# Turning and evicting the next head's query and key between the halves of the weight block, and behind the exponentials, in a two-block decoder kernel on one Trainium2 core

## The chip, the core and the metric

The kernel runs on one core of a Trainium2 chip. The metric is the device time of one execution in microseconds; it was run three times.

## The reference

Two stacks of blocks over 256 tokens of width 1024, in float32. The first stack has two layers. Each normalises its input, multiplies it with a wide weight matrix and computes heads: the even layer 8 differential attention heads (A: two softmaxes of 64 channels each, with ALiBi) and 4 cross attention heads over a memory (X); the odd layer 4 cross attention heads (Y) and 12 forgetting attention heads (C). The gated heads go through an output matrix and are added to the input. The heads that matter here:

```python
s1 = einsum('bhqd,bhkd->bhqk', q1b, k1) * scale + bias        # A, and s2 of the second halves
p1 = softmax(where(causal, s1, -inf)); p2 = softmax(where(causal, s2, -inf))
attn = p1 - lam * p2
o = einsum('bhqk,bhkd->bhqd', attn, v)
s = einsum('bhqd,bhkd->bhqk', qb, k) * scale                  # C
s = s + (cqb[..., :, None] - cum[:, :, None, :])
p = softmax(where(causal, s, -inf))
```

Queries and keys are normalised over the channels and have a gain per channel. The second stack (a recurrent and convolutional mixer, a pooling mixer, cross attention, two gated feed-forward blocks) follows; the change does not touch it.

## The kernel before, in words

All matrix products with weights are done three times over: a weight is split into a high part and a low part (w_hi, w_lo), as the activations are (u_s holds both parts), and high times high, high times low and low times high are summed in PSUM. A weight block (a "unit") is 1 MB. SP's queue loads it into w_raw (line 397), ScalarE copies it in two halves into w_hi (`hi`, line 1267), VectorE subtracts to get w_lo (`lo`, line 1908), and TensorE multiplies it in two halves. There are two buffers, so ScalarE works on block u+2 while TensorE multiplies block u: the first half of w_hi of block u+2 waits for TensorE's first half of block u, the second for its second half.

A unit has one of two forms. `k8_unit` (line 556) has 48 products of 256 columns and fills one bank, which ScalarE evicts at its end (line 1298, with Silu where the columns are a gate). `row_unit` (line 576) has 24 products of 512 columns; two such units make a pair, and their two banks are evicted in the second (line 1322). Both forms take a function `between`, which TensorE calls between the halves. The passes did not use it before the change. In both, a product with its three passes is lines 552, 553 and 554.

The two head passes ("e": heads 0 to 11, A then X; "o": heads 12 to 27, Y then C) run in slots. In the text slots are numbered by the number of their head, so that slots 0 to 16 are the first pass with its tail and slots 12 to 32 the second. In slot s every engine has an order written out by hand, and heads are at different stages:

- TensorE (`attention`, line 851): turn y of head s-5 (line 846), turn the probabilities of s-3 (line 804), scores of s-1 (lines 770 and 771 for A, 775 to 780 for C, 783 for X and Y), values of s-4 (lines 828 to 836), turn query and key of s (`st_turn_qk`, line 745), then the weight block of the slot. The scores wait for `a_qk`, the signal that ScalarE has evicted query and key of their head.
- ScalarE (`attention`, line 1512): y_hi of s-5 (line 1509), copy of the turned probabilities of s-3 (line 1480), squares of s-4 for A heads (line 1491), eviction of query and key of s (`st_qk`, lines 1443 and 1446; X and Y have a query only), first half of w_hi, exponentials of s-1 (`st_exp`, lines 1463, 1467, 1471), bank eviction, second half of w_hi. Exponential and Silu are in different function tables; a change between them is an ACT_TABLE_LOAD.
- VectorE (line 2227): y_lo of s-5 (lines 2196, 2200; waits for y_hi), combination of the probabilities of s-2 (lines 2141 to 2161), second half of w_lo, mask and maxima of s-1 (lines 2115 to 2127), gated head of s-4 (lines 2177, 2186), first half of w_lo.

Of the kernel before, what the change touches and what calls it, by code (L numbers as in the profile page):

```python
# [209 lines left out]
def build_program(nc, t, out):  # L210

    with ExitStack() as ctx:
# [52 lines left out]
        def tv(ap):  # L265
            return ap.rearrange("p (k n) -> p k n", n=SEQ)

        hv = two(h[:, :], D)
        uh, ul, yh_, yl_ = tv(u_hi), tv(u_lo), tv(y_hi[:, :]), tv(y_lo[:, :])
# [278 lines left out]
        def _(pe):  # L548
# [7 lines left out]
            def k8_unit(slot, bk, xh, xl, wait_lo, wait_bank, fresh=None, between=None):  # L556

                for half in range(2):  # L560
                    if fresh is not None:
                        pe.wait_ge(tL, fresh[half])
                    if half == 1 and between is not None:
                        between()
                    pe.wait_ge(lo_done, wait_lo + half)
                    if half == 0 and wait_bank is not None:
                        pe.wait_ge(evacuated, wait_bank)
                    for m in range(2):
                        for k in range(4 * half, 4 * half + 4):
                            a = 2048 * slot + SEQ * k + P * m  # L570
                            mm = passes(bank[bk][:, SEQ * m:SEQ * m + SEQ],
                                        ((w_hi[:, a:a + P], w_lo[:, a:a + P]), (xh[:, k, :], xl[:, k, :])),
                                        half == 0 and m == 0 and k == 0, k == 7)
                    mm.then_inc(half_done, 1)
# [22 lines left out]
            def row_of(name, j, xh, xl, fresh=None, between=None):  # L597

                u, kb = UNIT0[name] + j, BANK0[name] + j - j % 2
                first = j - j % 2  # L600
                row_unit(u % 2, j % 2, (unit_bank(name, first), unit_bank(name, first + 1)), xh, xl, 2 * u + 1,
                         kb - 1 if kb else None, fresh, between)
# [248 lines left out]
            def attention(name):  # L851
                lo, hi = PASS[name]
                for s in range(lo, hi + LAG):
                    for lag, stage in ((5, st_turn_y), (3, st_turn_p), (1, st_scores), (4, st_values), (0, st_turn_qk)):
                        if lo <= s - lag < hi:
                            stage(s - lag)
                    phase, before, count, out_name = BESIDE[name]
                    kind, j = beside(name, s)
                    u = beside_unit(name, s)
                    if kind == "K8":  # L860
                        kb = BANK0[phase] + j
                        if pair_of(phase, j) is None:
                            k8_unit(u % 2, kb % 2, uh, ul, 2 * u + 1, kb - 1)
                        else:
                            row_of(phase, j, uh, ul)
                    elif kind == "DN":
                        if j == 0:
                            pe.wait_ge(evacuated, BANK0[phase] + before + count)
                            pe.wait_ge(a_qk, hi)
                        pe.wait_ge(a_yl, lo + (A_HEADS if name == "e" and j == 0 else 2 * j + 2))  # L870
                        down_phase(out_name, j, 1)
# [178 lines left out]
            u, kb = UNIT0["e_nat"] + 14, BANK0["e_nat"] + 14  # L1050
# [29 lines left out]
            def turn_mem(m):  # L1080
                pe.wait_ge(nrm_ready, 5 + m)
                turn_tile(nrm, m)

            for j in range(2):
                u, kb = UNIT0["ab_t"] + j, BANK0["ab_t"] + j
                k8_unit(u % 2, kb % 2, uh, ul, 2 * u + 1, kb - 1,
                        fresh=(turned("h2", 3), turned("h2")) if j == 0 else None,
                        between=(lambda: turn_mem(0)) if j == 1 else None)
# [163 lines left out]
        def _(act):  # L1252
# [93 lines left out]
            def row_of(name, j, out_, between=None, after=None):  # L1346

                first = j - j % 2
                row_step(UNIT0[name] + j, j % 2, pair_of(name, j), (unit_bank(name, first), unit_bank(name, first + 1)), out_,
                         between=between, after=after)  # L1350
# [84 lines left out]
            def st_qk(g):  # L1435
                kind, hd = HEADS[g]
                if kind == "G":
                    return
                act.wait_ge(a_tr, g + 1)
                if g >= 2:  # L1440
                    act.wait_ge(a_sc, g - 1)
                qg = {"A": 0, "X": 1, "C": 2, "Y": 3}[kind]
                ins = act.activation(qk[g % 2][:, 0:SEQ], bank[TRB][:, 0:SEQ], ACT.Copy, scale=qs[:, qg:qg + 1])
                if kind in "AC":
                    kg = GCOL["ak" if kind == "A" else "ck"]
                    ins = act.activation(qk[g % 2][:, SEQ:512], bank[TRB][:, SEQ:512], ACT.Copy,
                                         scale=gT[:, kg:kg + 1])
                ins.then_inc(a_qk, 1)

            def st_exp(g):  # L1450
                kind, _ = HEADS[g]
                p = g % 2
                act.wait_ge(a_mx, g + 1)
                if kind in "XYG":
                    if g >= 2:
                        act.wait_ge(a_pt, g - 1)
                if g >= 2:
                    act.wait_ge(a_pn, g - 1)
                if kind == "A":
                    parts = [(c, m, Sb[p][:, 384 * c + P * m:384 * c + (P if m == 0 else 384)]) for c in range(2) for m in range(2)]  # L1460
                    for c, m, s in parts:
                        at = 2 * m + c
                        ins = act.activation(s, s, ACT.Exp, bias=nmax[p][:, at:at + 1], accum_out=rsum[p][:, at:at + 1])
                elif kind == "C":
                    for m in range(2):
                        s = Sb[p][:, P * m:P if m == 0 else 384]
                        ins = act.activation(s, s, ACT.Exp, bias=nmax[p][:, m:m + 1], accum_out=rsum[p][:, m:m + 1])
                else:
                    for m in range(2):
                        cs = slice(SEQ * m, SEQ * m + SEQ)  # L1470
                        ins = act.activation(Sb[p][:, cs], bank[SC[p]][:, cs], ACT.Exp, bias=nmax[p][:, m:m + 1],
                                             accum_out=rsum[p][:, m:m + 1])
                ins.then_inc(a_ex, 1)
# [38 lines left out]
            def attention(name):  # L1512
                lo, hi_ = PASS[name]
                for s in range(lo, hi_ + LAG):
                    for lag, stage in ((5, st_y_hi), (3, st_copy_p), (4, st_square), (0, st_qk)):
                        if lo <= s - lag < hi_:
                            stage(s - lag)

                    def exponentials():
                        if lo <= s - 1 < hi_:  # L1520
                            st_exp(s - 1)

                    kind, j = beside(name, s)
                    u = beside_unit(name, s)
                    phase, before, _, _ = BESIDE[name]
                    if kind is None:
                        exponentials()
                        continue
                    if kind == "K8" and pair_of(phase, j) is not None:
                        if name == "o" and j == 14:  # L1530
                            act.wait_ge(qk_ready, 4)
                        out_ = (row_out(eV, j // 2) if name == "e" else row_out(oK[:, :, 1024:], 0) if 18 <= j < 20
                                else row_out(oV, (14, 20, 24).index(j - j % 2)))
                        row_of(phase, j, out_, between=exponentials)
                        continue
                    if kind == "DN":
                        evac = None
                    elif name == "e":
                        evac = copy_out(t_dst(eXZ), 1, ACT.Silu) if j == 12 else \
                            copy_out(t_dst((eBH, eBC, eBB, eBZ)[(j - 4) // 2]), j % 2, ACT.Silu if j >= 10 else ACT.Copy)  # L1540
                    elif j < 14:
                        evac = copy_out(t_dst(oXZ), j - 12, ACT.Silu)
                    else:
                        evac = copy_out(t_dst(oZ), (16, 17, 22, 23, 26, 27).index(j), ACT.Silu)
                    step(u, evac, BANK0[phase] + j, between=exponentials)
# [131 lines left out]
            for j in range(OUT_TAIL["e"], 8):  # L1677
                u = UNIT0["e_out"] + j
# [1125 lines left out]
```

## Time and profile before

| what | value |
|---|---|
| median of 3 runs | 1329.51 us (1328.25 to 1330.42) |
| time of the profiled execution | 1328.74 us |
| its span in the trace | 1326.9 us |
| mean granted TensorE clock | 0.988 |
| busy: TensorE, VectorE, ScalarE | 96%, 68%, 52% of the span |
| chain that ended last | 76% TensorE, 12% VectorE, 5% ScalarE |

Times are read from the start of the span. In a timeline row the first number is the start of an instruction, the second its length; instructions overlap in their engine's pipeline, so the distance from one start to the next is what one occupies. A bracket at the end of a row says how long the engine was idle before it and what ended that.

### The profile page before, as it was taken

The page shows a single profiled execution, that of the slowest core. Times are in us where ns is not written, and L with a number is a line of the kernel's source. Part 1 is how long each engine was busy: PE and PEld are TensorE (multiplying, and loading weights), DVE is VectorE, ACT ScalarE, POOL GpSimd, SP SyncE. Part 2 cuts the span into 40 slices and gives each one's busy share as a digit, 9 for nine tenths or more (in the row PEclk, how much of TensorE's full clock was granted, in tenths as well). Part 3 has the DMA queues.
Part 4 walks back from the last instruction along what each step waited for, and adds up shares of the span by engine and source line. Part 5 has one row for each costly group of instructions (what it writes and reads, how often), then busy time and mean ns, then how long its engine had stood idle before and what let it go on. Part 6 is the DMA issues. An engine that isn't in the chain of part 4 may idle for free.

```text
span 1326.9 us, 19085 instructions
## 1 busy us (share of the span) xinstructions
PE 1273.1 (96%) x7208; PEld 1102.2 (83%) x7208; DVE 898.3 (68%) x1285; ACT 687.5 (52%) x1079; POOL 63.0 (5%) x72
## 2 busy tenths in 40 slices
PE   7999999999899999998989999999999998999997
PEld 6887899887788888897877988888887796888886
DVE  7676776775774655789786747666667646566667
ACT  6555777455567676457335444444443353444442
POOL 1012011000100000000000000000000000000000
PEclk9999999999999999999989999999999999999999
DMA  7655333555453434645335444566654453475652
GB/s 246 218 187 172 127 127 127 185 170 187 134 182 128 128 127 160 213 148 183 98 114 188 150 152 133 203 229 221 206 190 135 153 184 100 130 221 189 190 190 96
DMA packets 138525, 219.57 MB, mean 165 GB/s; under 512 B 3739, under 2 KB 92134, under 8 KB 138454
## 3 DMA queue, kind: packets, MB, share of 16 engines
q1 hardware_dynamic: 135110, 206.68, 47.2%
q0 software_dynamic: 3040, 11.19, 2.7%
q8 instruction: 47, 0.77, 0.2%
q10 hardware_dynamic: 304, 0.73, 0.2%
q14 instruction: 24, 0.20, 0.0%
HBM read 217.54 MB, written 1.05 MB: 165 GB/s over the span
## 4 chain that ended last, share of the span: by engine, by line
PE 76%; DVE 12%; ACT 5%; issue 3%; DMA 2%; POOL 1%; DVEq 0%; SPq 0%; ACTq 0%
PE bank L552 16%; PE bank L554 16%; PE bank L553 16%; PE bank L913 12%; PE bank L915 6%; DVE w_lo L1908 3%; ACT w_hi L1267 2%; DVE h L2065 1%; DVE small L2072 1%; PE bank L788 1%; PE bank L817 1%; PE bank L939 1%; PE bank L804 1%; DVE att L2553 1%; DVE att L1973 1%
## 5 line engine op out<-in xcount | busy, mean ns | idle before, releaser
L1908 DVE TENSOR_TENSOR w_lo<-w_raw,w_hi 128x1024 fp32r<-128x1024 f32 x388 | 471.9, 1224 | 268.8 <-ACT w_hi L1267 262.9
L1267 ACT ACTIVATE w_hi<-w_raw 128x1024 fp32r<-128x1024 f32 x388 | 408.1, 1059 | 431.9 <-PE bank L554 287.7
L913 PE MATMUL bank<-u_s,w_hi 128*128 128x512 f32 x672 | 239.1, 400 | 1.8 <-DVE u_s L2047 1.8
L552 PE MATMUL bank<-w_hi,y_hi 128*128 128x512 f32 x528 | 211.6, 401 | 5.9 <-DVE w_lo L1908 3.5
L554 PE MATMUL bank<-w_hi,y_lo 128*128 128x512 f32 x528 | 207.3, 393 | 0.0
L553 PE MATMUL bank<-w_lo,y_hi 128*128 128x512 f32 x528 | 207.0, 392 | 0.0
L915 PE MATMUL bank<-u_s,w_lo 128*128 128x256 f32 x672 | 189.1, 281 | 0.0
L552 PE MATMUL bank<-u_s,w_hi 128*128 128x256 f32 x544 | 157.4, 289 | 4.7 <-DVE u_s L2047 3.9
L913 PEld LDWEIGHTS bank<-u_s,w_hi 128*128 128x128 f32 x672 | 127.0, 189 | 33.3 <-DVE u_s L2047 2.0
L553 PE MATMUL bank<-u_s,w_hi 128*128 128x256 f32 x544 | 154.6, 284 | 0.0
L554 PE MATMUL bank<-u_s,w_lo 128*128 128x256 f32 x544 | 154.5, 284 | 0.0
L552 PE MATMUL bank<-w_hi,u_s 128*128 128x512 f32 x336 | 134.8, 401 | 10.9 <-DVE w_lo L1908 4.0
L553 PE MATMUL bank<-w_lo,u_s 128*128 128x512 f32 x336 | 132.2, 394 | 0.0
L554 PE MATMUL bank<-w_hi,u_s 128*128 128x512 f32 x336 | 132.0, 393 | 0.0
L915 PEld LDWEIGHTS bank<-u_s,w_lo 128*128 128x128 f32 x672 | 127.6, 190 | 0.7
L552 PEld LDWEIGHTS bank<-w_hi,y_hi 128*128 128x128 f32 x528 | 100.1, 190 | 29.8 <-DVE w_lo L1908 3.5
L554 PEld LDWEIGHTS bank<-w_hi,y_lo 128*128 128x128 f32 x528 | 99.8, 189 | 22.0
L553 PEld LDWEIGHTS bank<-w_lo,y_hi 128*128 128x128 f32 x528 | 100.2, 190 | 19.7
L552 PEld LDWEIGHTS bank<-u_s,w_hi 128*128 128x128 f32 x544 | 104.8, 193 | 6.0 <-DVE u_s L2047 4.6
L553 PEld LDWEIGHTS bank<-u_s,w_hi 128*128 128x128 f32 x544 | 105.0, 193 | 0.1
L554 PEld LDWEIGHTS bank<-u_s,w_lo 128*128 128x128 f32 x544 | 104.9, 193 | 0.0
L552 PEld LDWEIGHTS bank<-w_hi,u_s 128*128 128x128 f32 x336 | 63.8, 190 | 26.8 <-ACT nat L1322 5.5
(302 smaller groups left out, 1588.3 us busy)
## 6 DMA issues: line engine op xcount, KB each, us to landing
w_raw<-in_e_w_in SPq DMA_DIRECT2D x28, 1024.0 KB, 5.1
w_raw<-in_o_w_in SPq DMA_DIRECT2D x28, 1024.0 KB, 5.1
w_raw<-in_ffn_wg SPq DMA_DIRECT2D x22, 1024.0 KB, 5.4
w_raw<-in_ffn_wu SPq DMA_DIRECT2D x22, 1024.0 KB, 5.3
w_raw<-in_ffn_wd SPq DMA_DIRECT2D x22, 1024.0 KB, 4.9
w_raw<-in_ab_w_in SPq DMA_DIRECT2D x12, 1024.0 KB, 5.2
w_raw<-in_e_w_out SPq DMA_DIRECT2D x8, 1024.0 KB, 4.8
w_raw<-in_o_w_out SPq DMA_DIRECT2D x8, 1024.0 KB, 5.3
```

What stands on the lines that cost most here:

```text
L552: pe.matmul(out_ap, ah, bh, start=start, stop=False, skip_group_check=True)
L553: pe.matmul(out_ap, ah, bl, start=False, stop=False, skip_group_check=True)
L554: return pe.matmul(out_ap, al, bh, start=False, stop=stop_, skip_group_check=True)
L788: mm = pe.matmul(bank[SC[pr]][:, SEQ * m:SEQ * m + SEQ], XQT[:, 2 * hd + j, P * m:P * m + P], (KT2 if g < 32 else KT1)[:, 2 * hd + j, :], ...
L804: mm = pe.transpose(bank[PTB][:, dst:dst + P], s[:, src:src + P], ident)
L817: mm = pe.matmul(o[:, SEQ * j:SEQ * j + SEQ], V2[:, k, cs], p[:, SEQ * k:SEQ * k + SEQ], start=(k == 0), stop=(k == 1))
L913: pe.matmul(two(bank[banks[m]][:, :], SEQ), w_hi[:, a:a + P], u_both[:, :, SEQ * k:SEQ * k + SEQ], start=(k == 0), stop=False, skip_group_ ...
L915: mm = pe.matmul(bank[banks[m]][:, 0:SEQ], w_lo[:, a:a + P], uh[:, k, :], start=False, stop=(k == 7), skip_group_check=True)
L939: pe.matmul(o[:, :, ts], w_hi[:, a:a + P], u_both[:, :, SEQ * k + P * tile:SEQ * k + P * tile + P], start=(k == 0 and tile == 0), stop=Fal ...
L1267: act.activation(w_hi[:, at:at + 1024], w_raw[:, at:at + 1024], ACT.Copy).then_inc(hi_done, 1)
L1908: v.tensor_tensor(w_lo[:, at:at + 1024], w_raw[:, at:at + 1024], w_hi[:, at:at + 1024].bitcast(F32), ALU.subtract).then_inc(lo_done, 1)
L1973: mark(v.scalar_tensor_tensor(nrm[:, m], src[:, m], mv[:, m, 0:1], gain, ALU.subtract, ALU.mult))
```

## The change

In TensorE's program of both passes `st_turn_qk` of head s leaves the top of the slot and is called between the two halves of the slot's weight block. In ScalarE's program `st_qk` of head s leaves its place ahead of the first half of w_hi and stands behind the exponentials of head s-1, ahead of the bank eviction and the second half of w_hi. Every slot that turns a head has a weight block of the input projection, so all 28 heads are moved. VectorE's program and the queues of SP and GpSimd are as before.

```diff
--- before.py
+++ after.py
@@ -851,19 +851,26 @@
             def attention(name):
                 lo, hi = PASS[name]
                 for s in range(lo, hi + LAG):
-                    for lag, stage in ((5, st_turn_y), (3, st_turn_p), (1, st_scores), (4, st_values), (0, st_turn_qk)):
+                    for lag, stage in ((5, st_turn_y), (3, st_turn_p), (1, st_scores), (4, st_values)):
                         if lo <= s - lag < hi:
                             stage(s - lag)
+
+                    def next_head():
+                        if s < hi:
+                            st_turn_qk(s)
+
                     phase, before, count, out_name = BESIDE[name]
                     kind, j = beside(name, s)
                     u = beside_unit(name, s)
                     if kind == "K8":
                         kb = BANK0[phase] + j
                         if pair_of(phase, j) is None:
-                            k8_unit(u % 2, kb % 2, uh, ul, 2 * u + 1, kb - 1)
+                            k8_unit(u % 2, kb % 2, uh, ul, 2 * u + 1, kb - 1, between=next_head)
                         else:
-                            row_of(phase, j, uh, ul)
-                    elif kind == "DN":
+                            row_of(phase, j, uh, ul, between=next_head)
+                        continue
+                    next_head()
+                    if kind == "DN":
                         if j == 0:
                             pe.wait_ge(evacuated, BANK0[phase] + before + count)
                             pe.wait_ge(a_qk, hi)
@@ -1512,13 +1519,15 @@
             def attention(name):
                 lo, hi_ = PASS[name]
                 for s in range(lo, hi_ + LAG):
-                    for lag, stage in ((5, st_y_hi), (3, st_copy_p), (4, st_square), (0, st_qk)):
+                    for lag, stage in ((5, st_y_hi), (3, st_copy_p), (4, st_square)):
                         if lo <= s - lag < hi_:
                             stage(s - lag)
 
                     def exponentials():
                         if lo <= s - 1 < hi_:
                             st_exp(s - 1)
+                        if s < hi_:
+                            st_qk(s)
 
                     kind, j = beside(name, s)
                     u = beside_unit(name, s)
```

## Rows read from the trace of the kernel before

**Rows 1.** Windows of both passes: PE, PEld, DVE, ACT, POOL busy (instructions), clock, DMA.

```profile
120.00:235.00 115.00, 112.01 (x806) 101.01 (x805) 83.31 (x165) 84.22 (x201) 11.96 (x17) 1.00 0.40 131
375.00:508.00 133.00, 132.82 (x846) 116.80 (x845) 81.64 (x145) 95.76 (x178) 4.54 (x2) 1.00 0.41 132
```

**Rows 2.** Waits: total us, times, longest; the last row is of the second pass.

```profile
ACT w_hi L1267 <- PE bank L554: 17.4, 13, 2.0
...
PE bank L846 <- DVE att L2186: 0.9, 2, 0.6
...
PEld bank L552 <- ACT nat L1298: 0.8, 2, 0.5
```

**Rows 3.** Timeline of TensorE: block starts with and without transposes ahead.

```profile
122.50 0.28 PE L554 MATMUL bank<-u_s,w_lo 128*128 128x256 f32 x1
...
122.98 0.48 PE L552 MATMUL bank<-w_hi,u_s 128*128 128x512 f32 x1
...
447.34 0.38 PE L833 MATMUL bank<-att,nat 128*128 128x128 f32 x2
...
447.92 0.48 PE L552 MATMUL bank<-w_hi,u_s 128*128 128x512 f32 x1
...
514.01 0.38 PE L833 MATMUL bank<-att,nat 128*128 128x128 f32 x2
514.15 0.47 PE L552 MATMUL bank<-w_hi,y_hi 128*128 128x512 f32 x1
```

**Rows 4.** Timeline of ScalarE: eviction of query and key, first pass.

```profile
180.32 0.48 ACT L1443 ACTIVATE att<-bank,qs 128x256 f32<-128x256 f32 x1 [0.17 <-ACT att L1491]
180.69 0.47 ACT L1446 ACTIVATE att<-bank,gT 128x256 f32<-128x256 f32 x1
```

**Rows 5.** Timeline: slots with a table load, second pass, last C and first Y.

```profile
387.98 1.03 PE L783 MATMUL bank<-mkv,att 128*128 128x256 f32 x4
...
388.21 0.46 ACT L1471 ACTIVATE att<-bank,small 128x256 f32<-128x256 f32 x1
...
503.41 1.28 ACT L1467 ACT_TABLE_LOAD   x1
504.70 0.41 ACT L1467 ACTIVATE att<-att,small 128x128 f32<-128x128 f32 x1
...
505.11 0.49 ACT L1467 ACTIVATE att<-att,small 128x256 f32<-128x256 f32 x1
...
505.28 0.39 PE L775 MATMUL bank<-att 128*128 128x128 f32 x2
```

**Rows 6.** Timeline: a C slot without a table load.

```profile
443.95 0.49 ACT L1467 ACTIVATE att<-att,small 128x256 f32<-128x256 f32 x1
...
445.40 0.39 PE L775 MATMUL bank<-att 128*128 128x128 f32 x2
```

**Rows 7.** Timeline: slot 1 of the first pass and the next block start.

```profile
135.56 0.50 PE L770 MATMUL bank<-att 64*128 64x128 f32 x4
...
137.14 1.06 ACT L1322 ACTIVATE nat<-bank 128x512 f32<-128x512 f32 x2
...
137.86 0.47 PE L552 MATMUL bank<-w_hi,u_s 128*128 128x512 f32 x1 [0.79 <-ACT nat L1322]
```

**Rows 8.** Timeline: one period of slots 7 and 8, first pass.

```profile
184.49 0.40 ACT L1463 ACTIVATE att<-att,small 128x128 f32<-128x128 f32 x1 [1.52 <-DVE small L2120]
...
186.26 0.57 ACT L1298 ACTIVATE nat<-bank 128x512 f32<-128x512 f32 x1
...
188.18 0.48 DVE L2196 SCALAR_TENSOR_TENSOR y_lo<-bank,qs,y_hi 128x256 fp32r<-128x256 f32 x1 [2.08 <-ACT y_hi L1509]
...
192.81 0.68 DVE L2120 TENSOR_REDUCE small<-att 128x2 f32<-128x512 f32 x1
...
193.52 0.40 ACT L1463 ACTIVATE att<-att,small 128x128 f32<-128x128 f32 x1 [1.76 <-DVE small L2120]
...
194.66 1.03 PE L783 MATMUL bank<-mkv,att 128*128 128x256 f32 x4
```

## The prediction

> **What bounds the kernel now.** I first read the windows of the two head passes [rows 1]. The reader is to see that TensorE is busy for 112.01 of 115 us in the first pass and 132.82 of 133 us in the second, at the full granted clock: TensorE's instruction stream sets the time here, so whatever makes TensorE wait is paid in full, and moving its own work about gains nothing by itself. The waits view [rows 2] says what little waiting there is. TensorE waits 0.9 us for VectorE's gated heads (L2186) and, in the second pass, its weight loads 0.8 us for a bank that ScalarE has not emptied. ScalarE waits 17.4 us in the first pass, in 13 pieces, for the first half of a weight block. The evictions of query and key stand today just ahead of that wait. They are hidden in it, and the change takes them out of it. Last I read the timelines slot by slot (a slot is the head work and one weight block).
>
> **TensorE's part.** The transposes (four for an A or C head, two for X and Y) are neither added nor removed. At the boundary, from the last value product to the block's first product, it is 447.34 to 447.92 = 0.58 us with them and 514.01 to 514.15 = 0.14 without: they cost 0.44. Between products of a block: 122.50 to 122.98 is 0.48, less the ordinary 0.12 from one product to the next, 0.36; the first product behind them takes some 0.09 longer than the others, so 0.45 [rows 3]. The difference is 0.01 a slot; I take nothing, with bounds of 0 and 0.1 for each of 28 slots, 0 to 2.8 us. What does change is that the transposes now stand ahead of the next scores instead of behind the last ones, so that the scores come 0.45 later (0.20 with two transposes) after the half of the block that lets ScalarE begin. That is the only cover that the move gives.
>
> **ScalarE's part.** The two evictions start 0.37 apart (180.32, 180.69), so they occupy 0.75 us, and the second ends 0.85 after the first began; with about 0.05 for the semaphore the scores can start 0.90 after the evictions begin [rows 4]. An X or Y head has one: 0.38 of occupancy, 0.53 to the scores. They move past the first half of the weights' high part and past the exponentials, and these now stand behind them in ScalarE's queue: the bank eviction, the second half of the high part, y_hi and the copy of the probabilities. New is that the scores of head s, at the top of slot s+1, follow directly on exponentials plus evictions. Three kinds of slot come out of this.
>
> (a) Slots with a table load ahead of the exponentials, because the block before was gated with Silu. Second pass, last such slot: load at 503.41, exponentials from 504.70 to 505.11 + 0.49 = 505.60, scores possible at 506.50; TensorE gets there at 505.28 + 0.45 = 505.73, so it waits 0.77 [rows 5]. There are five of this kind with C heads, 0.66 to 0.93 each, 4.05 in all by the same subtraction. Two have Y heads; the first: exponentials end at 388.21 + 0.46 = 388.67, scores at 389.20 against 387.98 + 0.20 = 388.18, a wait of 1.02 [rows 5]; the other gives 0.73. Together 5.8. A later block start swallows waits for banks that exist today, 0.5 of the 0.8 in [rows 2]. Second pass: +5.3. C slots without a load have room: exponentials end at 443.95 + 0.49 = 444.44, scores possible at 445.34, TensorE there at 445.40 + 0.45 = 445.85 [rows 6]: no wait, 0.51 to spare.
>
> (b) First pass, slots 1 to 3. In slot 1 the exponentials end at 137.14 (there the bank's eviction starts), so the scores start at 138.04 instead of 135.56 + 0.45 = 136.01: 2.03 of waiting. Behind these scores TensorE waits today for the bank, 0.79 by the row and about 1.0 with what the sequencer adds [rows 7]; that is swallowed, net +1.0. In slots 2 and 3 the exponentials of an A head take 1.77 (184.49 to 186.26) where those of a C head take 0.90 (504.70 to 505.60) [rows 5, 8], so the 0.51 to spare becomes a wait of 0.36: +0.7 for the two. Slot 4 has a longer block and a turned y ahead of its scores: nothing.
>
> (c) First pass, slots 5 to 8: a ring between ScalarE and VectorE. The exponentials start at 184.49 and again at 193.52, a period of 9.03 (three equal ones in a row) [rows 8]. Inside it each step starts as the last ends: exponentials to 186.26, bank eviction, second high half, y_hi; VectorE's y_lo at 188.18, held 2.08 by y_hi; combine, low half, mask and maxima until 192.81 + 0.68 = 193.49; exponentials at 193.52 [rows 8]. The evictions are not in this ring today; the change puts 0.75 us into it. VectorE's 2.08 idle is no cover, for it ends with y_hi, which comes later. So 9.78 a period. The ring is entered 2.0 late (1.7 from (b), and 0.3 because it starts sooner behind the evictions), three periods add 2.25, and the last exponentials, ending today at 193.52 + 1.77 = 195.29, end at 199.5; with one query eviction the scores start at 200.1 instead of 194.66 [rows 8]: 5.4 late in all. One more load slot with an X head, slot 11, gives 0.35 by the way of (a). First pass: +5.8.
>
> Late second halves of w_lo and the weight loads that SP starts behind them move by the same amounts; a block is needed a whole slot later, so they are covered, and POOL's queue has nothing moved past it.
>
> **The sum.** 5.8 + 5.3 = 11.1, and 0.4 of the 0 to 2.8 from TensorE's switching: +11.5. Against the profiled execution's own time, 1328.74 (span 1326.9), that is 1340.2. The median of the runs shown is 0.77 above that execution: 1329.51 + 11.5 = 1341.0.
>
> **A rule against the trace.** A load takes 1.28 and the exponentials begin 1.29 after it began (503.41, 504.70) [rows 5]. The Trainium skill, "ScalarE: Activation LUTs", section "What ACT_TABLE_LOAD costs", counts a drain of some 1.38 us on top of a load of 1.28. By that rule the seven waits of (a) would be 9.7 us longer and the sum an estimated 21; the row shows no such drain, and I go by the row.
>
> **The rivals.**
> Only the load slots pay (chance 0.12): VectorE has slack in the ring that I don't see, and (c) adds nothing beyond (b). Then 1.0 + 0.7 + 0.35 + 5.3 = 7.3, 1336.8. For it: VectorE is idle 2.08 each period. Against: the releaser of that idle is y_hi [rows 8].
> All slots pay (0.08): the 0.51 to spare of a C slot is not there, and the eight C and Y slots without a load wait some 0.4 too, and switching costs 0.1 a slot: 11.1 + 3.2 + 2.8 = 17.1, 1346.6. Against: the arithmetic of [rows 6].
> No measurable change (0.04): the exponentials are released earlier because ScalarE reaches the first high half without the evictions ahead of it, and this makes up for the 0.75. It decides if the first high half waited for ScalarE; but ScalarE waits there for TensorE, 17.4 us in 13 pieces [rows 2]. It would give 1329.5 to 1331.
> Faster (0.03): the ring does not close over y_hi but over VectorE's use of the first high half, so that taking the evictions from ahead of it shortens the ring, and TensorE's present waits, 0.9 for L2186, 0.8 at the banks and 1.0 in slot 1 [rows 2, 7], disappear: 1326.8. It decides if VectorE's long wait in a slot ends with w_hi instead of y_hi.
>
> **How the numbers follow.** The forecast has 0.73. About 0.2%, 2.7 us, is what a measurement of this kernel can tell from no change. The range goes from 1335 (a little below the load-slot case) to 1347 (the case in which all pay). It also holds the sum with each of the 15 waits off by 0.3 us, 4.5, and leaves out only the last two rivals and some of the tails. Slower 0.93, same 0.04, faster 0.03.
>
> **What the changed profile would show.** Right: TensorE's scores (L770, L775, L783) waiting for ScalarE's L1446 or L1443 in slots 1 to 3, 5 to 8 and the load slots, about 0.3 to 2 us each; starts of the exponentials 9.8 apart where they are 9.03; no such wait in C slots without a load; no wait for L2186 left in the first pass; the second pass 5 us longer and the first 6. Wrong: the period still near 9.03, or the scores of the load slots following the transposed probabilities at once. If the scores wait in the plain C slots too, the dear rival holds.

## The result and the profile after

| | before | after |
|---|---|---|
| median of the runs | 1329.97 us (1328.25 to 1331.73, 4 runs) | 1338.99 us (1338.14 to 1340.25, 4 runs) |
| time of the profiled execution | 1328.74 us | 1338.14 us |
| its span | 1326.9 us | 1336.3 us |
| mean granted TensorE clock | 0.988 | 0.989 |

The changed kernel is slower: the ratio of after to before is 1.0072, with a 95% interval of 1.0059 to 1.0085, that is 7.8 to 11.3 us. The forecast was 1341.0 with a range of 1335 to 1347. In a second comparison with more rounds, shown below, the ratio was 1.0084 (1.0070 to 1.0098), 9.3 to 13.0 us.

The waits of TensorE in the changed kernel, total us, times and longest; the first two rows are of the first pass, the last two of the second.

```profile
PE bank L770 <- ACT att L1453: 6.0, 6, 1.9
PE bank L783 <- ACT att L1450: 1.1, 2, 1.0
...
PE bank L775 <- ACT att L1453: 3.0, 5, 0.7
PE bank L783 <- ACT att L1450: 1.3, 2, 0.8
```

Lines 1450 and 1453 are lines 1443 and 1446 of before: the evictions of query and key. In the kernel before none of these waits existed. What stood there, 0.9 us for the gated heads and the waits at the banks [rows 2], is gone from the two windows, except the 1.3 us at the last block start of the first pass. TensorE now waits 7.1 us in the first pass and 4.3 in the second, in 8 and 7 places, always for the eviction of the head whose scores come next. Behind such a wait the first scores of a C, X or Y head also take 0.1 us longer: 516.12 to 516.45 below is 0.33 where 453.51 to 453.74 in a slot without a wait is 0.23. The first scores of an A head take 0.32 in either kernel.

The ring of slots 5 to 8, timeline of ScalarE and VectorE, the period that answers to [rows 8]; the last row is TensorE's scores, which belong near its start:

```profile
186.90 0.40 ACT L1470 ACTIVATE att<-att,small 128x128 f32<-128x128 f32 x1 [1.29 <-DVE small L2129]
...
188.18 0.49 ACT L1470 ACTIVATE att<-att,small 128x256 f32<-128x256 f32 x1
188.68 0.45 ACT L1450 ACTIVATE att<-bank,qs 128x256 f32<-128x256 f32 x1
189.03 0.46 ACT L1453 ACTIVATE att<-bank,gT 128x256 f32<-128x256 f32 x1
189.39 0.58 ACT L1305 ACTIVATE nat<-bank 128x512 f32<-128x512 f32 x1
189.87 1.05 ACT L1274 ACTIVATE w_hi<-w_raw 128x1024 fp32r<-128x1024 f32 x1
190.81 0.46 ACT L1516 ACTIVATE y_hi<-bank,qs 128x256 fp32r<-128x256 f32 x1
...
191.31 0.48 DVE L2205 SCALAR_TENSOR_TENSOR y_lo<-bank,qs,y_hi 128x256 fp32r<-128x256 f32 x1 [2.79 <-ACT y_hi L1516]
...
195.94 0.68 DVE L2129 TENSOR_REDUCE small<-att 128x2 f32<-128x512 f32 x1
...
196.66 0.40 ACT L1470 ACTIVATE att<-att,small 128x128 f32<-128x128 f32 x1 [1.29 <-DVE small L2129]
...
189.54 0.50 PE L770 MATMUL bank<-att 64*128 64x128 f32 x4 [1.23 <-ACT att L1453]
```

Each step of the chain from 186.90 to 196.66 starts as the one before it ends. The exponentials now start 9.76 apart; before it was 9.03. What came in is the two evictions, 188.68 to 189.39 = 0.71. VectorE's idle time ahead of y_lo grew from 2.08 to 2.79, by the same 0.71: it did not shrink to take the evictions in, so it was no cover. The scores at 189.54 start when the second eviction, 189.03 + 0.46 = 189.49, is done.

A load slot, the last of the second pass (it answers to [rows 5]), and a plain C slot ([rows 6]):

```profile
451.58 0.49 ACT L1474 ACTIVATE att<-att,small 128x256 f32<-128x256 f32 x1
...
452.44 0.46 ACT L1453 ACTIVATE att<-bank,gT 128x256 f32<-128x256 f32 x1
...
453.51 0.39 PE L775 MATMUL bank<-att 128*128 128x128 f32 x2
453.74 0.60 PE L776 MATMUL bank<-att 128*128 128x256 f32 x2
...
513.07 1.28 ACT L1474 ACT_TABLE_LOAD   x1
514.36 0.40 ACT L1474 ACTIVATE att<-att,small 128x128 f32<-128x128 f32 x1
514.76 0.49 ACT L1474 ACTIVATE att<-att,small 128x256 f32<-128x256 f32 x1
515.26 0.45 ACT L1450 ACTIVATE att<-bank,qs 128x256 f32<-128x256 f32 x1
515.61 0.46 ACT L1453 ACTIVATE att<-bank,gT 128x256 f32<-128x256 f32 x1
...
515.04 0.49 PE L804 MATMUL bank<-cst,att 128*128 128x128 f32 x3
516.12 0.49 PE L775 MATMUL bank<-att 128*128 128x128 f32 x2 [0.59 <-ACT att L1453]
516.45 0.60 PE L776 MATMUL bank<-att 128*128 128x256 f32 x2
```

In the plain slot the eviction is done at 452.90 and the scores come at 453.51, 0.61 later. Less the 0.05 from an eviction's end to the scores, as at 189.49 and 189.54 above, that is 0.56 to spare, where the forecast had 0.51. In the load slot it is done at 516.07, while TensorE had finished the turned probabilities (three transposes from 515.04) and was idle for 0.59.

**How the loss lies.** The start of each head's scores can be compared between two profiles, counted from the first head of the pass; heads are numbered within their pass. In the first pass the shift grows by 2.05 at head 1 and has fallen to 1.53 at head 2, as the wait for the bank behind it went; then it is 1.86 at head 3, 1.85 at 4, and 3.04, 4.13, 4.87 and 5.32 at heads 5 to 8; it is 5.72 at the last. In the second pass it grows at the seven load slots by 0.98, 0.37, 0.63, 1.04, 0.74, 1.03 and 0.74, 5.5 in all, and by 0.5 elsewhere, to 6.07. That is 11.8 us in the two passes, of which the block start at the end of the second gives 0.2 back. The spans differ by 9.4 only. The rest is outside the passes: the first head's scores began at 127.57, 1.05 us earlier than before, at a place where the kernels do not differ but for the order of one head's transposes and evictions, and 1.1 us came back between 570 and 684 us. The first does not repeat in a second profile of the changed kernel, the second does; the experiments and the last section have more of both.

### The profile page after: what moved, and what is told of

Its sections match the earlier page's. It is cut to its first block, busy times and chain, and to the rows that moved or that the text cites. A ratio compares the mean times of both kernels' runs of the same rounds, so it can differ in the third digit from the quotient of the medians.

```text
span 1336.3 us, 19085 instructions
## 1 busy us (share of the span) xinstructions
PE 1272.5 (95%) x7208; PEld 1100.1 (82%) x7208; DVE 898.4 (67%) x1285; ACT 684.7 (51%) x1079; POOL 63.1 (5%) x72
## 3 DMA queue, kind: packets, MB, share of 16 engines
HBM read 217.54 MB, written 1.05 MB: 164 GB/s over the span
## 4 chain that ended last, share of the span: by engine, by line
PE 73%; DVE 14%; ACT 6%; issue 3%; DMA 2%; POOL 1%; DVEq 0%; ACTq 0%; SPq 0%
PE bank L552 15%; PE bank L554 15%; PE bank L553 15%; PE bank L920 12%; PE bank L922 6%; DVE w_lo L1917 4%; ACT w_hi L1274 2%; DVE h L2074 1%; DVE att L2562 1%; DVE small L2081 1%; PE bank L788 1%; PE bank L817 1%; ACT att L1470 1%; PE bank L946 1%; DMA w_raw<-in_ab_w_in 1%
```

## The experiments

Each time is compared with that of the kernel before on the same chip. The ratio is worked out over the single runs and is not the quotient of the two medians shown. The diffs of TensorE's edit alone, of the order ahead of the exponentials and of the single passes are against the changed kernel, that of ScalarE's edit alone and that of the copies against the kernel before; the other two edits were made to both. "In the profile" is the shift of the scores against the profile of before, counted as above, first pass and second pass.

**The change again.**

> The change once more, timed in more rounds and with a second profile. Ring theory (evictions behind the exponentials sit between the exponentials and the next scores, and in a ring between ScalarE and VectorE): 11 us over the kernel before inside the two passes, 9 to 11.5 us in the whole, since parts outside the passes differ by about 1 us from one execution to the next. In the profile TensorE's scores wait some 8.5 us for the key or query eviction in the first and 4 us in the second pass. Rival (the whole is the 9.0 us of the first comparison because something outside the passes got faster by 2): the profile repeats a part outside the passes that is shorter than before.

Measured: 1341.06 us against 1329.25, ratio 1.0084 (1.0070 to 1.0098). In the profile +5.68 and +6.01, and TensorE's wait rows are the same four to the digit. The shift inside the passes repeats to 0.1 us. The scores of the first head began at 129.17 here, and over the profiles of this study, all with the same program up to there but for head 0, between 127.57 and 130.43: this is what one execution differs by from another, and it was not a part that the change had made faster. Between 570 and 684 us, however, this profile is again 1.2 us shorter than that of before, as the first one was by 1.1. To that extent the rival holds: a part outside the passes was shorter in both profiles of the changed kernel. It gives back a tenth of the loss, and the last section says what is seen there. Behind 695 us this execution then lost another 2.2 us, which the first did not. The 8.5 us of waits that this expectation gave for the first pass were too many: 7.1 were measured in either profile.

**Which of the two edits costs.** TensorE's alone, then ScalarE's alone:

```diff
 # pe_only: ScalarE as in the kernel before
-for lag, stage in ((5, st_y_hi), (3, st_copy_p), (4, st_square)):
+for lag, stage in ((5, st_y_hi), (3, st_copy_p), (4, st_square), (0, st_qk)):
...
                     def exponentials():
                         if lo <= s - 1 < hi_:
                             st_exp(s - 1)
-                        if s < hi_:
-                            st_qk(s)
```

> TensorE turns between the halves, but ScalarE evicts where it did, ahead of the first high half. Ring theory: the scores never wait for the eviction; the evictions now start some 0.5 us after TensorE's first half and delay the first high half by 1 us, which the exponentials of the ring slots absorb; three block starts that wait for a bank (slots 1 and 13 and the end of the second pass) wait about 0.7 us longer: +2 to +3 us over the kernel before. Rival (TensorE's extra switches between products and transposes cost the time): +9 us, as the whole change.

Measured: 1333.74 against 1329.25, ratio 1.0032 (1.0021 to 1.0043), that is +2.8 to +5.7. In the profile +1.77 and +0.73. The block starts that wait for a bank, timeline of TensorE, slot 1 and the two of the second pass:

```profile
138.59 0.47 PE L552 MATMUL bank<-w_hi,u_s 128*128 128x512 f32 x1 [2.00 <-ACT nat L1329]
...
393.50 0.50 PE L552 MATMUL bank<-w_hi,u_s 128*128 128x512 f32 x1 [0.63 <-ACT nat L1305]
...
511.53 0.50 PE L552 MATMUL bank<-w_hi,y_hi 128*128 128x512 f32 x1 [0.72 <-ACT nat L1305]
```

The wait of slot 1 was 0.79 [rows 7] and is 2.00; the others are as expected. No scores wait. The scores of the passes do not show all of the cost: the block start behind the second pass adds 0.67, and 0.66 lies between the passes, where profiles differ by up to that much without an order that could be told. Of the first pass's 1.77, 1.1 come at the bank and 0.5 at heads 5 and 6, where the ring is entered later; the expectation had the ring absorb all of it. Turning between the halves does not cost nine microseconds, but it is not free where ScalarE keeps its place, since the eviction then holds up the first high half and all behind it.

```diff
 # act_only: TensorE as in the kernel before
-for lag, stage in ((5, st_y_hi), (3, st_copy_p), (4, st_square), (0, st_qk)):
+for lag, stage in ((5, st_y_hi), (3, st_copy_p), (4, st_square)):
...
                         if lo <= s - 1 < hi_:
                             st_exp(s - 1)
+                        if s < hi_:
+                            st_qk(s)
```

> TensorE turns at the top of the slot as before, ScalarE evicts behind the exponentials. Ring theory: all of the change's cost, and the 0.45 us of cover that the transposes gave between the halves is missing in every slot that waits outside the ring: 9 to 11 us plus 0.45 in slots 1 to 3 and five load slots, 0.2 in two or three, and a first small wait in the plain C slots: +13 to +16 us over the kernel before. Rival (TensorE's placement is what costs): no more than +2 us.

Measured: 1347.10 against 1329.25, ratio 1.0130 (1.0111 to 1.0149), +14.8 to +19.8. In the profile +8.78 and +8.49. ScalarE's edit alone costs more than both together. The second pass is 2.4 us dearer than with both, the five C load slots at 0.45 and two Y at 0.2 (2.65) as expected. The first pass is 3.1 dearer where 1.5 had been expected. What was left out is mainly the clock behind slot 1. TensorE's waits in the first pass, and its timeline behind the longest of them:

```profile
PE bank L770 <- ACT att L1446: 7.6, 7, 2.4
PE bank L783 <- ACT att L1443: 1.3, 2, 1.0
...
139.25 0.81 PE L770 MATMUL bank<-att 64*128 64x128 f32 x4 [2.38 <-ACT att L1446]
139.83 1.07 PE L771 MATMUL bank<-att 64*128 64x256 f32 x4
140.83 1.11 PE L745 MATMUL bank<-cst,nat 128*128 128x128 f32 x4
141.60 0.78 PE L552 MATMUL bank<-w_hi,u_s 128*128 128x512 f32 x1
```

After 2.38 us of idle time the granted clock is 0.50 from 139 to 142 us, the lower level (1.2 GHz). The two score products start 0.58 apart and the transposes 1.00 later, where the kernel before has 0.32 and 0.54 in the same slot (135.56, 135.88, 136.42). The transposes and the block's first product then take 0.77 and 0.57, where they take 0.36 and 0.31 at the full clock, so that some 1.4 us are lost here. In the changed kernel the wait of slot 1 is 1.91 and the granted clock stays at 1.00.

So, once ScalarE evicts behind the exponentials, the transposes between the halves help: they give the evictions 0.45 us of cover. By themselves they cost, as the run before shows.

**Ahead of the exponentials instead of behind them.**

```diff
                     def exponentials():
-                        if lo <= s - 1 < hi_:
-                            st_exp(s - 1)
                         if s < hi_:
                             st_qk(s)
+                        if lo <= s - 1 < hi_:
+                            st_exp(s - 1)
```

> TensorE turns between the halves, ScalarE evicts behind the first high half but ahead of the exponentials. Ring theory: the scores no longer wait; the exponentials come 0.75 us later, which the ring slots absorb (they wait 0.6 to 1.8 us for VectorE there); the three block starts behind banks pay 0.75 each: +2 to +3 us over the kernel before. Rival (any eviction in the second half of a slot costs, wherever it stands): +9 us as the change.

Measured: 1331.48 against 1329.25, ratio 1.0020 (1.0011 to 1.0030), +1.5 to +4.0. In the profile +1.03 and +0.56, with no scores that wait, 1.6 us at the bank behind slot 1 and 0.9 for gated heads as before. The same evictions in the same half of the slot, one place earlier in ScalarE's queue, cost 1.6 us at the scores of the two passes instead of 11.8. It is the place behind the exponentials that costs, by both its consequences, for in this order the exponentials' wait for VectorE covers the 0.75 us in the ring.

**Pass by pass.**

```diff
+                    if name != "e" and s < hi:
+                        st_turn_qk(s)
...
                     def next_head():
-                        if s < hi:
+                        if name == "e" and s < hi:
                             st_turn_qk(s)
 # and the same for st_qk on ScalarE; "o" in the other kernel
```

> Both edits in the first pass alone. Ring theory: the 5.7 us that the first pass lost in the profile of the changed kernel, +5 to +6.5 us over the kernel before. Rival (the two passes' losses are one, passed on): near +11.

> Both edits in the second pass alone, where there is no ring and every wait should stand in a slot with a table load. Theory: the 6.0 us less 0.2 of the profile, +5 to +6.5 us over the kernel before. Rival (the cost is the first pass's ring alone): +0 to +1.

Measured: first pass alone 1334.84 against 1329.35, ratio 1.0044 (1.0028 to 1.0060); second alone 1334.25, ratio 1.0032 (1.0019 to 1.0045). In the profiles +5.68 and -0.05, and 0.00 and +6.04. The two losses are independent and add up. The second one's median is below what its profile shows, 2.5 to 6.0 us by the interval.

**Opening the ring from VectorE's side.**

```diff
                     phase, before, count, _ = BESIDE[name]
-                    for lag, stage in ((5, st_y_lo), (2, st_combine)):
+                    for lag, stage in ((2, st_combine), (5, st_y_lo)):
```

> The kernel before, with VectorE's combination of the probabilities ahead of y_lo in both passes. This opens the ring: VectorE starts as the exponentials end and does not wait for y_hi first. Ring theory: slots 5 to 8 fall from up to 9.03 us to TensorE's own 8.46, 1.2 us in all: -1 to -1.5 us against the kernel before, and no wait of TensorE for a gated head in the first pass. Rival (the period of 9.03 is not set by that ring): 0.

> The changed kernel with the same reordering on VectorE. Ring theory: the evictions stand no more in a ring, and the waits of slots 5 to 8 (4.7 us over TensorE's own time) go; slots 1 to 3, 11 and the load slots stay: 4.5 to 5 us less than the changed kernel, +5.5 to +6.5 us over the kernel before. Rival (the scores of slots 5 to 8 wait because the evictions stand behind the exponentials at all, ring or not, as in the load slots): less than 1 us under the changed kernel, +10 or more.

Measured: on the kernel before, 1326.72 against 1329.35, ratio 0.9974 (0.9964 to 0.9985), 2.0 to 4.8 us faster; on the changed kernel 1336.72, ratio 1.0049 (1.0035 to 1.0063), where the changed kernel itself had 1.0084 and 1.0072. In the profiles -1.54 and -0.05, and +0.57 and +6.01. Starts of the exponentials in the kernel before with this edit, timeline of ScalarE:

```profile
165.99 0.38 ACT L1463 ACTIVATE att<-att,small 128x128 f32<-128x128 f32 x1
...
174.45 0.38 ACT L1463 ACTIVATE att<-att,small 128x128 f32<-128x128 f32 x1
...
182.91 0.38 ACT L1463 ACTIVATE att<-att,small 128x128 f32<-128x128 f32 x1
```

The measured gain, 2.0 us at least, is somewhat more than the 1.6 that the passes show and than the 1 to 1.5 that were expected; where the rest lies was not found. The period is 8.46, TensorE's own, and the exponentials no longer wait for VectorE (no bracket). The waits of TensorE in the changed kernel with it, first pass:

```profile
PE bank L770 <- ACT att L1453: 2.4, 3, 1.9
PE bank L552 <- ACT nat L1305: 1.3, 1, 1.3
PE bank L783 <- ACT att L1450: 0.2, 1, 0.2
```

Six waits of the A heads have become three, those of slots 1 to 3, and of the X heads' two the one of slot 11 is left. The evictions still stand behind the exponentials, but no ring passes through them. In slots 5 to 8 the cost was the ring.

**Taking the table loads away.** Both kernels with the gates of the second pass left without Silu:

```diff
-evac = copy_out(t_dst(oXZ), j - 12, ACT.Silu)
+evac = copy_out(t_dst(oXZ), j - 12)
...
-evac = copy_out(t_dst(oZ), (16, 17, 22, 23, 26, 27).index(j), ACT.Silu)
+evac = copy_out(t_dst(oZ), (16, 17, 22, 23, 26, 27).index(j))
```

> The kernel before with Copy in place of Silu in the bank evictions of the second pass (its gates are not activated), so that ScalarE changes tables no more in its slots. Two block starts behind banks lose their waits: 0 to -0.7 us against the kernel before. Rival (table loads cost the kernel before on the path): -5 us or more.

> The changed kernel with the same Copy in place of Silu in the second pass. Load theory: no exponentials start behind a table load there, so the scores do not wait and the second pass costs what it did; the first pass keeps its 5.7: +5 to +6.5 us over the kernel before, some 5.5 us less than the changed kernel. Rival (the scores wait because of the eviction's 0.75 us alone, load or not): +10 us or more over the kernel before.

Measured: before with it 1327.13 against 1329.56, ratio 0.9983 (0.9973 to 0.9993); the changed kernel with it 1337.10, ratio 1.0062 (1.0049 to 1.0075), +6.5 to +10.0. In the profiles -0.02 and -0.46, and +5.65 and +0.92. TensorE's waits in the second pass of the latter come down to one row:

```profile
PE bank L783 <- ACT att L1450: 0.8, 1, 0.8
```

That one is slot 13, the first exponentials of the pass, whose load stays. The five waits of C heads are gone with their loads, and the second pass's loss goes from 6.0 to 0.9 + 0.5 = 1.4 us. The profile confirms the load theory. The times do so less well. The kernel before without the loads is 0.9 to 3.6 us faster by the interval, where its profile shows 0.5 in the pass and 0.3 at the block start behind it. The changed kernel without the loads costs 8.2 us by its ratio, more than the 5 to 6.5 that were expected and 1.6 above the 6.6 of its own profile's passes, which lie at the lower end of its interval. The first pass keeps its loads in both; slot 1 has one too (132.63 to 133.91 in the changed kernel), and how much of its 2 us that load makes was not taken apart.

**Copies that nobody waits for, in the ring.**

```diff
                         if lo <= s - 1 < hi_:
                             st_exp(s - 1)
+                        if name == "e" and 5 <= s <= 8:
+                            for n in range(2):
+                                act.activation(nat[:, 13312 + 256 * n:13568 + 256 * n],
+                                               cst[:, 256 * n:256 * n + 256], ACT.Copy)
```

> The kernel before, with two copies of 256 columns behind the exponentials of slots 5 to 8 of the first pass, as long as the evictions that the change puts there; nobody waits for them, and the scores depend on nothing new. Ring theory: the periods of the exponentials grow from 9.03 by the copies' length in three slots, +2 to +3 us over the kernel before. Rival (the changed kernel loses in slots 5 to 8 only because the scores wait for the evictions, and there is no ring): 0 to +0.3.

Measured: 1330.46 against 1329.56, ratio 1.0013 (1.0004 to 1.0023), +0.5 to +3.1. In the profile +2.04 and -0.05. The starts of the exponentials:

```profile
168.24 0.40 ACT L1463 ACTIVATE att<-att,small 128x128 f32<-128x128 f32 x1 [0.59 <-DVE small L2123]
...
177.89 0.40 ACT L1463 ACTIVATE att<-att,small 128x128 f32<-128x128 f32 x1 [1.77 <-DVE small L2123]
...
187.53 0.40 ACT L1463 ACTIVATE att<-att,small 128x128 f32<-128x128 f32 x1 [2.14 <-DVE small L2123]
```

The period is 9.65, 0.62 over the 9.03 of before, though the scores depend on nothing new. TensorE then waits for the gated heads (2.7 us) where in the changed kernel it waits for the eviction.

## Why the prediction was right, point by point

**TensorE's part**: shown, near zero. With TensorE's edit alone no slot of the second pass without a bank wait grew by more than 0.06 us, 0.23 in all (0.50 at head 2 to 0.73 at the last). The 0.4 that the sum set aside for it was a choice between bounds of 0 and 2.8, and was of the right size. The 0.45 us of cover is what the second pass lost by its removal (2.4 us against 2.65).

**(a), load slots**: 5.8 less 0.5 were forecast. The seven slots cost 5.5, one by one 0.98, 0.37, 0.63, 1.04, 0.74, 1.03, 0.74 where the subtraction gave 1.02, 0.45 (0.73 less 0.28), 0.66, 0.93, 0.77, 0.92, 0.77. That the load is the reason is shown by the kernel without Silu. A further 0.5 us, forecast as nothing, lies in the other slots, at most 0.2 in one. Together 6.1, less 0.2 at the end of the pass, where 5.3 was forecast.

**(b), slots 1 to 3**: the wait of slot 1 was forecast as 2.03; its scores came 2.05 later, with 1.91 of idle time in the trace, and the bank's wait was swallowed as forecast. In slots 2 and 3 TensorE waited 0.35 and 0.16 where 0.36 each was forecast. Forecast +1.7 up to slot 4, measured 1.85.

**(c), the ring**: shown by opening it from the other side, by loading it with idle copies, and by the period, 9.76 for a forecast 9.78. The ring was entered 2.01 late (167.39 for 166.43, and the pass began 1.05 earlier) for a forecast 2.0. The scores of head 8 came 5.3 late where 5.4 had been forecast, and the whole first pass 5.7 for 5.8.

**The sum**: 11.5 was forecast and 11.6 is what the two passes lost (5.7 + 6.1 - 0.2). That they agree to 0.1 is in part luck: the second pass lost 5.9 where 5.3 was forecast, which the 0.4 set aside for TensorE's switching, and 0.1 too much in the first pass, nearly made up. The whole kernel lost 7.8 to 11.3 us in one comparison and 9.3 to 13.0 in the other. The forecast of 1341.0 lies 2.0 us above the first median and 0.1 below the second. What the first lacked lies outside the passes, for which the forecast had nothing: in its profiled execution 1.05 us ahead of them, which does not repeat, and 1.1 behind them, which does. That the second median lies on the forecast is luck too, since executions of one program spread over more than 3 us.

**The table-load rule**: the row was followed, and the trace stays with it. Exponentials follow a load's start by 1.29 (513.07, 514.36), with no drain to be seen; the load itself starts 0.02 behind the end of ScalarE's instruction ahead (511.99 + 1.06 = 513.05). The seven slots cost what the subtraction without a drain had given.

**The rivals**: "only the load slots" falls, as the ring paid; "all slots pay" falls, as the plain C slots have 0.6 to spare; "no change" and "faster" fall with the releaser that [rows 8] named. The faster one had half a point: a ring does set slots 5 to 8, and opening it does make the kernel before faster. It does not close over the first high half, but over y_hi.

## What to carry to other kernels

Work that is moved into an engine's idle time has to be placed by what follows it in that engine's queue, and not only by how full the slot is: 0.75 us of evictions stood ahead of a wait for TensorE in the kernel before, cost 1.6 us at the scores of the passes directly ahead of the exponentials, and 11.8 directly behind them. Where the starts of one instruction are evenly spaced at more than the bounding engine's own period, look for a ring of two other engines; idle time that lies inside the ring is no cover, and swapping two independent steps on one of them may open it. Here that is one line on VectorE, and the kernel before with it beats both kernels: 1326.72 us, ratio 0.9974 (0.9964 to 0.9985).

## What was not expected of the hardware

How much TensorE's clock falls after nearly the same wait differs from one profiled execution to the next. Around 608 us of the kernel before TensorE waits 1.5 and 2.2 us for a bank; around 618 us of the changed kernel it waits 1.7 and 2.0 us at the same two instructions. Stretches of 4 us behind these waits, first of the kernel before, with the granted clock third from the end:

```profile
612.00:616.00 4.00, 4.00 (x12) 3.07 (x11) 3.85 (x5) 1.06 (x1) 0.00 (x0) 0.62 0.38 145
616.00:620.00 4.00, 4.00 (x22) 3.33 (x21) 4.00 (x9) 1.06 (x1) 0.00 (x0) 1.00 0.79 245
```

and after:

```profile
622.00:626.00 4.00, 4.00 (x19) 3.30 (x18) 3.85 (x4) 1.46 (x3) 0.00 (x0) 1.00 0.59 226
626.00:630.00 4.00, 4.00 (x24) 3.39 (x23) 4.00 (x9) 1.01 (x1) 0.00 (x0) 1.00 0.53 168
```

In the kernel before the clock was at its lower level (1.2 GHz) for most of the first 4 us, and TensorE got through 12 products where it got through 19 after. This makes up the 1.1 us that came back between 570 and 684 us. Whether the change has a part in it is open. From 600 to 640 us the mean granted clock is 1.00 in five of the thirteen profiles: both of the changed kernel, those of the two single passes, and that with the evictions ahead of the exponentials. It is 0.96 in the kernel before, and 0.91 or 0.96 in the seven others, among them the changed kernel with VectorE's swap and without Silu, and the kernel before with copies. The five share no edit that the others all lack, and there is only one profile of the kernel before as it is.

Why the first head's scores start at 127.57 in one execution and at 130.43 in another can be read in the timelines of TensorE's first weight block, behind a wait of 1.3 us. First the kernel before with the copies, which starts at 130.43, then the changed kernel:

```profile
16.40 0.63 PE L554 MATMUL bank<-w_hi,y_lo 128*128 128x512 f32 x1
16.83 0.63 PE L552 MATMUL bank<-w_hi,y_hi 128*128 128x512 f32 x1
...
11.75 0.40 PE L553 MATMUL bank<-w_lo,y_hi 128*128 128x512 f32 x1
11.98 0.40 PE L554 MATMUL bank<-w_hi,y_lo 128*128 128x512 f32 x1
```

In the first the products start 0.43 apart, which is their distance at 612 to 615 us of the kernel before, where the granted clock is 0.50; in the second 0.23. The first 14 products are slow in the one and none in the other; in the kernel before, which starts at 128.62, the first six are. Fourteen times 0.20 is 2.8 of the 2.9 us. The granted clock of the profile reads 1.00 in this stretch of all three, so that it is the distance of the products that tells, and what decides how many are slow was not tried.

These two stretches are most of why a comparison of medians can't settle one microsecond here, while shifts inside the passes repeat to 0.1.
